# Second and third feed-forward: high weights meet both input parts in one product of 512 columns, each output tile in a bank of its own, halves added from SBUF

## The reference

```python
def swiglu(h, w_gu, w_down):
    gate, up = jnp.split(h @ w_gu, 2, axis=-1)
    return (jax.nn.silu(gate) * up) @ w_down

x = x + swiglu(rms_norm_2(x, a_norm2_g[i]), a_ffn_gu[i], a_ffn_down[i])   # second, tag f2
x = x + swiglu(rms_norm_2(x, b_norm2_g[j]), b_ffn_gu[j], b_ffn_down[j])   # third, tag f3
return rms_norm_2(x, final_norm_g)
```

## Time and profile before

| | us |
|---|---|
| median of 3 runs | 1126.77 (1126.12 to 1126.94) |
| the profiled execution: time | 1124.54 |
| the profiled execution: span | 1122.7 |
| f2 up part on TensorE (first product to last) | 617.24 to 741.4 |
| f2 down part | 741.4 to 804.2 |
| f3 up part | 927.13 to 1051.3 |
| f3 down part | 1051.3 to 1113.3 |

### The profile page before, as it was taken

One profiled execution on the slowest core, in us unless ns is written; L12 is line 12 of the kernel. 1 busy time (PEld: TensorE's weight loads), 2 busy tenths in 40 slices (PEclk: granted clock), 3 DMA queues, 4 the chain that ended last, 5 costly groups with the idle time before them and its releaser, 6 DMA issues.

```text
span 1122.7 us, 23982 instructions
## 1 busy us (share of the span) xinstructions
PE 1052.3 (94%) x10514; PEld 1001.3 (89%) x10514; DVE 750.3 (67%) x1232; ACT 555.6 (49%) x828; POOL 0.9 (0%) x7
## 2 busy tenths in 40 slices
PE   4999999799999999998788999999999999999997
PEld 4988889798899997986668999999988899999996
DVE  6799758778787657977645655566657755555654
ACT  5246364555456548744233544444557646444442
POOL 0000000000000000000000000000000000000000
PEclk9989999899999999999999999999999999999999
DMA  8858555244465553422002555445514435554451
GB/s 354 333 219 305 186 185 219 82 188 188 188 231 196 201 225 115 151 78 76 5 3 76 188 188 188 153 158 187 189 33 149 148 146 178 191 188 160 154 183 38
DMA packets 30378, 185.90 MB, mean 166 GB/s; under 512 B 3377, under 2 KB 4673, under 8 KB 12865
## 3 DMA queue, kind: packets, MB, share of 16 engines
q1 hardware_dynamic: 30272, 184.36, 45.1%
HBM read 183.29 MB, written 1.05 MB: 164 GB/s over the span
## 4 chain that ended last, share of the span: by engine, by line
PE 73%; DVE 14%; DMA 4%; ACT 4%; issue 3%; SPq 0%; DVEq 0%; ACTq 0%
PE banks L355 39%; PE banks L1253 16%; DVE wlo L315 4%; DMA raw<-in_w_up 3%; PE banks L352 3%; PE banks L335 2%; ACT whi L300 2%; DVE adac L522 2%; DMA con<-in_cons 1%; DVE S L522 1%; PE banks L1790 1%; PE banks L1797 1%; DMA raw<-in_a_in 1%; PE banks L575 1%; PE banks L1780 1%
## 5 line engine op out<-in xcount | busy, mean ns | idle before, releaser
L315 DVE TENSOR_TENSOR wlo<-raw,whi 128x2048 fp32r<-128x2048 f32 (+3 forms) x167 | 332.4, 1991 | 198.9 <-ACT whi L300 198.9
L300 ACT ACTIVATE whi<-raw 128x2048 fp32r<-128x2048 f32 (+3 forms) x167 | 278.4, 1669 | 171.6 <-PE banks L1253 77.5
L355 PE MATMUL banks<-h_hi,whi 128*128 128x256 f32 x1424 | 193.4, 289 | 6.9 <-ACT h_hi L2040 3.6
L355 PEld LDWEIGHTS banks<-h_hi,whi 128*128 128x128 f32 x1424 | 180.4, 194 | 12.0 <-issue 5.3
L355 PE MATMUL banks<-h_hi,wlo 128*128 128x256 f32 x1424 | 184.8, 282 | 0.3
L355 PE MATMUL banks<-h_lo,whi 128*128 128x256 f32 x1424 | 184.8, 281 | 0.1
L355 PEld LDWEIGHTS banks<-h_hi,wlo 128*128 128x128 f32 x1424 | 174.9, 189 | 2.5 <-issue 1.2
L355 PEld LDWEIGHTS banks<-h_lo,whi 128*128 128x128 f32 x1424 | 173.2, 187 | 3.5 <-issue 2.6
L1279 ACT ACTIVATE u<-u 128x256 f32<-128x256 f32 x44 | 18.4, 418 | 128.9 <-DVE u L1333 128.8
L1253 PE MATMUL banks<-m_lo,whi 128*128 128x256 f32 x528 | 75.2, 281 | 0.0
L1253 PE MATMUL banks<-m_hi,whi 128*128 128x256 f32 x528 | 75.1, 280 | 0.0
(11 more groups left out here) (449 smaller groups left out, 1391.0 us busy)
## 6 DMA issues: line engine op xcount, KB each, us to landing
raw<-in_ada SPq DMA_DIRECT2D x24, 1024.0 KB, 5.2
raw<-in_w_up SPq DMA_DIRECT2D x22, 1024.0 KB, 6.5
raw<-in_a_gu SPq DMA_DIRECT2D x22, 1024.0 KB, 4.8
raw<-in_b_gu SPq DMA_DIRECT2D x22, 1024.0 KB, 4.8
raw<-in_w_in SPq DMA_DIRECT2D x12, 1024.0 KB, 6.5
raw<-in_w_down SPq DMA_DIRECT2D x16, 704.0 KB, 4.1
raw<-in_a_in SPq DMA_DIRECT2D x11, 1024.0 KB, 5.1
raw<-in_a_down SPq DMA_DIRECT2D x16, 704.0 KB, 4.0
```

Source lines behind the costliest of these rows:

```text
L300: act.activation(hi_s[k % NSPLIT][:, 0:w], raw[n % NRAW][:, 0:w], ACT.Copy).then_inc(*hi_made.tick(k))
L315: dve.tensor_tensor(lo_s[s][:, 0:w], raw[n % NRAW][:, 0:w], hi_s[s][:, 0:w].bitcast(F), SUB).then_inc(*lo_made.tick(k))
L355: i_ = pe.matmul(b[0:m, j * T:(j + 1) * T], a[:, kt * step + j * m:kt * step + j * m + m], x[:, kt, :], start=st, stop=sp)
```

## The change

The high and low inputs are laid side by side (`hh`, `mm`), so that one product of 512 columns gives high W by high x in the first 256 columns of a bank and high W by low x in the next 256. The product of low W by high x adds to the first 256. So an output tile fills a bank; a chunk of the up part takes two banks (`two_banks[i % 4]`, all eight banks in turn). Before anything else is done with an output tile, its two halves are added: ScalarE copies the second halves from PSUM to SBUF (`second`) and VectorE adds the first halves to them (`sum`). In the up part this is one operation of 512 columns on each engine for both tiles of the chunk, in the down part one of 256 for each f. The scaling and `mul` then read SBUF. Chunk 0 of the up part goes kt by kt over all its products. The first feed-forward (`w_up`) keeps its products of 256 columns.

The core of the diff:

```diff
-        h_hi = sb("h_hi", [P, 8, T], R, hx, "right")
-        h_lo = sb("h_lo", [P, 8, T], R, hx, "right")
+        hh = sb("hh", [P, 8, 2, T], R, hx, "right")
+        h_hi, h_lo = hh[:, :, 0, :], hh[:, :, 1, :]
...
+        def both(x, kt):
+            return x[:, kt, :, :].rearrange("p a t -> p (a t)")
+        def pe_chunk_both(pe, name, i, bb, x, first=None):
+            k = split_k[name, i]
+            hi, lo = hi_s[k % NSPLIT], lo_s[k % NSPLIT]
+            pe.wait_ge(*hi_made.at(k))
+            turns = [(n, kt, j) for n in range(2) for j in range(2) for kt in range(8)]
+            if first is not None:
+                pe.wait_ge(*lo_made.at(k))
+                turns = [(n, kt, j) for kt in range(8) for n in range(2) for j in range(2)]
+            for o, (n, kt, j) in enumerate(turns):
+                w = slice(kt * 256 + j * P, kt * 256 + j * P + P)
+                if n == 0:
+                    if first is not None and j == 0:
+                        first(pe, 0, kt)
+                        first(pe, 2, kt)
+                    pe.matmul(bb[:, 512 * j:512 * j + 512], hi[:, w], both(x, kt), start=kt == 0, stop=False)
+                else:
+                    if o == 16:
+                        pe.wait_ge(*lo_made.at(k))
+                    x_ = pe.matmul(bb[:, 512 * j:512 * j + 256], lo[:, w], x[:, kt, 0, :], start=False, stop=kt == 7)
+            x_.then_inc(*chunk_done.tick(k))
...
-        m_hi = sb("m_hi", [P, 22, T], R, s2)
-        m_lo = sb("m_lo", [P, 22, T], R, s2)
+        mm = sb("mm", [P, 22, 2, T], R, s2)
+        m_hi, m_lo = mm[:, :, 0, :], mm[:, :, 1, :]
...
+                if up != "w_up":
+                    if i < 2:
+                        pe.wait_ge(*x_made.at((before, 4 * i + 3)))
+                    elif i == 2:
+                        pe.wait_ge(*rs_a.at((before, "ln")))
+                    elif i > 3:
+                        pe.wait_ge(*up_v.at((tag, "sum", i - 4)))
+                    pe_chunk_both(pe, up, i, two_banks[i % 4], hh, wait_h("n" + tag) if i == 0 else None)
+                    if i == 0:
+                        pe_mean(pe, before, bank[4])
+                    continue
...
-                elif up == "w_up":
+                else:
...
-                else:
-                    pe.wait_ge(*up_v.at((tag, "mul", i - 4)))
...
-                if i == 0 and up != "w_up":
-                    pe_mean(pe, before, bank[4])
...
+                if up != "w_up" and f in (0, 2):
+                    pe.wait_ge(*up_v.at((tag, "sum", 18 + f // 2)))
...
+                    parts = 3 if up == "w_up" else 2
...
-                        turns = [(n, kt) for kt in range(11) for n in range(3)]
+                        turns = [(n, kt) for kt in range(11) for n in range(parts)]
...
-                        turns = [(n, kt) for n in range(3) for kt in range(11)]
+                        turns = [(n, kt) for n in range(parts) for kt in range(11)]
...
-                        if f == 0 and n == 2:
+                        if f == 0 and n == (2 if up == "w_up" else 0):
...
+                        if up != "w_up" and n == 0:
+                            pe.matmul(b[:, :], a[:, kt * P:kt * P + P], both(mm, 11 * half + kt),
+                                      start=half == 0 and o == 0, stop=False)
+                            continue
...
+                        act.wait_ge(*done_at(up, i))
+                        if i >= NU:
+                            act.wait_ge(*m_lo_v.at((tag, i - NU)))
+                        act.activation(z[:, :, :], two_banks[i % 4][:, :].rearrange("p (j a t) -> p j a t", j=2, a=2)[:, :, 1, :],
+                                       ACT.Copy).then_inc(*up_a.tick((tag, "second", i)))
...
-                        act.activation(z[:, 1, :], z[:, 1, :], ACT.Silu).then_inc(*up_a.tick((tag, "silu", i)))
+                        act.activation(z[:, 0, :], z[:, 0, :], ACT.Silu).then_inc(*up_a.tick((tag, "silu", i)))
...
+                if up != "w_up":
+                    act.wait_ge(*done_at(down, 2 * f + 1))
+                    act.activation(ub[:, f, :], bank[4 + f % 4][:, T:2 * T], ACT.Copy).then_inc(*up_a.tick((tag, "second", 22 + f)))
...
-                        dve.wait_ge(*done_at(up, i))
+                        halves = two_banks[i % 4][:, :].rearrange("p (j a t) -> p j a t", j=2, a=2)
+                        dve.wait_ge(*up_a.at((tag, "second", i)))
+                        dve.tensor_tensor(z[:, :, :], halves[:, :, 0, :], z[:, :, :], ADD).then_inc(*up_v.tick((tag, "sum", i)))
...
-                        dve.tensor_tensor(z[:, 1, :], b[:, 0:T], rs_t[:, :], MUL).then_inc(*up_v.tick((tag, "rs", i)))
+                        dve.wait_ge(*up_v.at((tag, "sum", i)))
+                        dve.tensor_tensor(z[:, 0, :], z[:, 0, :], rs_t[:, :], MUL).then_inc(*up_v.tick((tag, "rs", i)))
...
-                    z, b = u[(i - 1) % NU], bank[(i - 1) % 4]
+                    z = u[(i - 1) % NU]
...
-                    other = z[:, 0, :] if up == "w_up" else b[:, T:2 * T]
-                    dve.tensor_tensor(z[:, 0, :], other, z[:, 1, :], MUL).then_inc(*up_v.tick((tag, "mul", i - 1)))
+                    dve.tensor_tensor(z[:, 0, :], z[:, 0, :], z[:, 1, :], MUL).then_inc(*up_v.tick((tag, "mul", i - 1)))
...
-                    dve.tensor_tensor(ub[:, f, :], b[:, 0:T], rs_t[:, :], MUL).then_inc(*ub_v.tick(key))
+                    dve.wait_ge(*up_a.at((tag, "second", 22 + f)))
+                    dve.tensor_tensor(ub[:, f, :], b[:, 0:T], ub[:, f, :], ADD).then_inc(*ub_v.tick((key, "sum")))
+                    dve.wait_ge(*ub_v.at((key, "sum")))
+                    dve.tensor_tensor(ub[:, f, :], ub[:, f, :], rs_t[:, :], MUL).then_inc(*ub_v.tick(key))
```

## The result

The changed kernel takes 1160.91 us (median of 4 runs, 1158.18 to 1162.65), the kernel before 1126.44 beside it. The ratio is 1.0307, with a 95% interval of 1.0283 to 1.0331: 3% slower. A second set of runs on another occasion gave 1.0320 (1.0299 to 1.0341). The profiled execution of the changed kernel took 1160.2 us with a span of 1158.4, so the spans are 35.7 us apart.

A forecast was written before the change was run, and what follows sets the result against it. It took a VectorE-ScalarE ring of 5.58 us to match TensorE's 5.60 per chunk. 14.8 + 14.8 + 2.8 + 0.9 + 1.6 = 34.9 us on 1126.8 gave 1161.7 us, 8 in 10 range 1148 to 1172.

The forecast's parts named there:

- f2: `m_lo` of chunk 21: End of f2's up part: later start and 21 longer steps, less two used-up waits, make this operation 15.05 us later.
- f2: to the end of the second half chunk: Start of f2's down part: the first output tile's second half needs `m_lo` of all chunks, +14.8 us.
- f2: the other 14 half chunks: Rest of f2's down part: TensorE sets the time, VectorE and ScalarE have room for their additions, no change.
- exit of f2: End of f2: copy behind the weight split, then `sum`, scaling and addition; positions requested later, +2.8 us.
- f3: to the end of the second half chunk: f3's up part and start of its down part: same trace as f2, so +14.8 us.
- exit of f3: End of f3: no weight splits left, copy 0.46 and `sum` 0.46, +0.9 us.
- The ring: Up parts: closed cycle of waits over VectorE and ScalarE grows by 0.72 to 6.30 us a chunk, against TensorE's 5.60.
- the rival that VectorE had room by its share of busy time: Up parts: VectorE's 2.29 us idle time per step takes the `sum`, all sets gain 0.010; 1122.1 us, 5% chance.
- The wide product: TensorE: 512 columns take 0.233 us, a set 0.350 as before, no gain; rival fixed cost of 0.010, 13%.
- The copy: Up parts: ScalarE's 0.59 us copy lies in its idle time and costs nothing; rival not covered, 1188.6 us, 7%.
- the entries: Start of each up part: TensorE needs the low input earlier in its products, so starts 1.1 us later, 2 x 1.1.
- The clock: TensorE's waits at the ends of up parts: one clock fall on the path for both feed-forwards together, +1.6 us.

The follow-up runs named there:

- The two places of the same operation: Kernel before plus one unused 512-column VectorE operation from PSUM per up step of f2 and f3: ahead of the scaling 1157.26 us, behind it 1128.18 us.
- the cut ring: Changed kernel with ScalarE's high weights of chunk i+3 moved ahead of the Silu of chunk i: 1132.58 us, ratio 1.0049 to the kernel before.
- the last run above: Kernel before with only ScalarE's high weights moved ahead of the Silu: 1125.51 us, ratio 1.0008.
- the run that holds the clock: Changed kernel plus 34 unused 256-column products in TensorE's idle time around each down part's second half chunk: 1161.65 us, against 1164.6 for the changed kernel.

## Why the prediction was right

Term by term, by the shifts between the two profiled executions. Ahead of f2 the changed kernel is 0.25 us early (VectorE's first low input at 617.59, it was 617.84).

| term | forecast, us | measured, us |
|---|---|---|
| f2: `m_lo` of chunk 21 | 15.05 | 763.34 - 748.58 + 0.25 = 15.0 |
| f2: to the end of the second half chunk | 14.8 | 764.26 - 749.22 + 0.25 = 15.3 |
| f2: the other 14 half chunks | 0, with the clock 0.8 | 0.9 |
| exit of f2 | 2.8 | 2.8 |
| the layer between | 0 | -0.5 |
| f3: to the end of the second half chunk | 14.8 | 15.3 |
| f3: the other 14 half chunks | 0, with the clock 0.8 | 1.2 |
| exit of f3 | 0.9 | 0.9 |
| less the lead ahead of f2 | | -0.25 |
| sum (without the first row, which the second contains) | 34.9 | 35.7 |

**The ring.** Right in place and size. That the `sum` is paid in full, 0.72 a step, rests on one reading: VectorE's idle time lay inside the ring and not before the scaling. The two places of the same operation and the cut ring show it. Its own mark in the trace, scalings 6.30 apart, came out at 6.31 to 6.32. The two places also answer the rival that VectorE had room by its share of busy time.

**The wide product.** Right: 0.350 a set. The earlier trace rows gave 0.18 for 384 columns where a fixed cost would have given 0.170; 512 columns take 0.233. From 256 to 384 to 512 columns the time is proportional to the columns, 0.1167, about 0.175 (0.173 to 0.178 in the trace of the kernel before) and 0.233. The formula of the Trainium skill ("TensorE: Matmul & The Clock Gate", Back-to-back issue gap), which the page gives for isolated products and which makes 0.216 of 512 columns, does not agree with this trace (0.233). In the down parts a half chunk of wide and narrow products takes 3.88 us at the full clock. With narrow products alone it takes 3.92 in f2 and 3.87 in f3 of the kernel before, but 3.92 in both when only the order of ScalarE's work changes (the last run above). So with the same narrow products a half chunk differs by 0.05 us from one place and execution to another. The prediction had put such a difference down to addresses; here the buffers are the same, and its cause is open.

**The copy.** Covered, as forecast; in the run without the `sum` it stays, and what it costs can't be told from the entries.

**The clock.** The mechanism was right, the count was not: I took one fall for both feed-forwards, and there are two on the path. In f2 the stretch view of the changed kernel shows it:

```profile
760.90:764.30 3.40, 2.46 (x7) 1.75 (x8) 1.13 (x4) 3.00 (x4) 0.00 (x0) 0.50 0.63 212
```

Each fall costs 1.5 to 2.2 us by the run that holds the clock, so 3 to 4 us in all where the sum has 1.6. A part of it lies in the second half chunk: with the clock held that one ends 14.9 us later than in the kernel before, counted from f2's low inputs (768.74 - 622.42 against 749.22 - 617.84), as forecast, and 15.3 without. That the sum came out only 0.8 short is in part luck: it had nothing for f2's half chunks of 3.88 in place of 3.92 (-0.5), the layer between (-0.5, cause open) and the lead ahead of f2 (-0.25).

**A detail that was wrong.** I had TensorE stopped by the low weights from about chunk 15. It waits for the *high* weights, before the first product of a chunk, and its rows with such a wait are eight in each feed-forward, chunks 14 to 21; chunk 13 already starts 0.2 us late. With the wide products first in a chunk it has 3.73 us between needing the one and the other, while they are made 2.29 us apart; the high weights come late first. It changed nothing in the sum, since the ring's own length sets the end.

What is left open: f2 starts up to 6 us apart from one trace to another, for the changed kernel (616.6 to 622.4) and the one before (616.9 to 620.5) with their variants, and this goes with the time at half clock ahead of it. That the clock is the cause was not tested: I did not try to hold it there.

## What to carry to other kernels

Before adding an operation to an engine that is "58% busy", find out where its idle time lies. Idle time inside a cycle of waits between two engines is no room: write down the period of the cycle and compare it with the bound engine's. Here an operation put where the engine waits anyway cost nothing that could be measured, and the same operation ahead of what the other engine waits for cost its full price. The cure was to let the other engine do its independent work before the dependent one. And before merging products to save a cost per product, look for one product of another width in the trace: here, though only one row, already pointed to no such cost.

## What the runs showed of the hardware that I had not expected

The time of an `fp32r` product at the full clock is about 9% above its columns at 2.4 GHz for each of three widths in these traces (0.1167, about 0.175 and 0.233 us for 256, 384 and 512 columns, the first and last from the up parts; 256 columns take 0.119 in f2's down part before the change), while at the half clock it is its columns at 1.2 GHz (0.214 us for 256).
